# Second block's attention: turned queries and keys straight from the products, two heads at a time on parts of TensorE's array

## What is computed

```python
def odd_mixer(h_lat, h_ctx, ...):             # 256 tokens and 256 context tokens
    z = h @ w_in                               # latents cq (384), ckv (256), shared kr (32), gates
    q = (rms_norm(cq) @ w_uq).reshape(n, 8, 64 + 32)     # nope 64, rope 32 columns
    q = concat(q[..., :64], rope(q[..., 64:]))
    kv = (rms_norm(ckv) @ w_ukv).reshape(512, 8, 64 + 64)
    k = concat(kv[..., :64], broadcast(kr, 8 heads))     # one rotated part for all heads
    v = kv[..., 64:]
    p = softmax(q @ k.T * 96 ** -0.5)          # 256 queries, 512 keys, 8 heads
    o = p @ v                                  # 8 x 64 columns
    return concat(o, gb * conv(gc * hh)) @ w_out
```

## Time and profile before

| what | value |
|---|---|
| time, median of 3 runs | 2270.16 us |
| the 3 runs | 2269.73, 2270.16, 2275.33 us |
| span of the profiled execution | 2267.3 us |
| PE busy | 1983.1 us, 87% of the span |
| DVE busy | 999.4 us, 44% |
| ACT busy | 750.1 us, 33% |
| read from memory | 640.31 MB, 283 GB/s over the span |

### The profile page before, as it was taken

How to read it: one execution, slowest core, us unless ns; L and a number is a source line. 1 busy time by engine, 2 the same in 40 slices (tenths; PEclk the granted TensorE clock), 3 DMA queues, 4 the chain that set the end, 5 groups by cost and what they waited for, 6 DMA issues and landing times.

```text
span 2267.3 us, 37964 instructions
## 1 busy us (share of the span) xinstructions
PE 1983.1 (87%) x16424; PEld 1484.3 (65%) x16424; DVE 999.4 (44%) x1906; ACT 750.1 (33%) x1336; POOL 14.4 (1%) x30
## 2 busy tenths in 40 slices
PE   6999899989898999765565668999999999999998
PEld 5778765444444767544444445878888878788886
DVE  3445522222221656311101105655677756557776
ACT  3344400000000645100000004655455456655544
POOL 0000000000000000000000000000000000000000
PEclk9999999999999999888878878999999999999999
DMA  9868489999999445799999996434545543355551
GB/s 404 334 251 345 148 346 428 428 427 426 428 427 426 170 149 223 282 425 427 427 426 425 427 423 254 149 118 181 203 174 192 196 163 144 118 191 213 195 191 56
DMA packets 49203, 643.79 MB, mean 284 GB/s; under 512 B 5600, under 2 KB 5872, under 8 KB 10256
## 3 DMA queue, kind: packets, MB, share of 16 engines
q1 hardware_dynamic: 46080, 624.56, 68.4%
q0 software_dynamic: 2960, 16.82, 1.9%
HBM read 640.31 MB, written 1.05 MB: 283 GB/s over the span
## 4 chain that ended last, share of the span: by engine, by line
PE 64%; DMA 28%; DVE 4%; ACT 2%; issue 2%; SPq 0%; DVEq 0%; ACTq 0%
PE bank L985 61%; DMA ring<-in_stream 28%; PE bank L993 3%; ACT ring L1921 0%; ACT weights_high L1734 0%; DVE ring L2507 0%; DVE weights_low L2765 0%; ACT tokens_high_low L2085 0%; DVE arena L2865 0%; ACT arena L1767 0%; ACT arena L1756 0%; ACT arena L2051 0%; DVE odz_low L2259 0%; DVE tokens_low L2617 0%; DVE arena L2216 0%
## 5 line engine op out<-in xcount | busy, mean ns | idle before, releaser
L985 PE MATMUL bank<-ring,arena 128*32 128x128 f32 (+5 forms) x7668 | 618.3, 379 | 201.9 <-DMA ring<-in_stream 194.5
L985 PEld LDWEIGHTS bank<-ring,arena 128*32 128x32 f32 (+2 forms) x7668 | 371.1, 135 | 420.3 <-DMA ring<-in_stream 204.8
L2765 DVE TENSOR_TENSOR weights_low<-ring,weights_high 128x1024 fp32r<-128x1024 f32 (+2 forms) x288 | 343.3, 1193 | 257.6 <-ACT weights_high L1734 254.8
L1734 ACT ACTIVATE weights_high<-ring 128x1024 fp32r<-128x1024 f32 (+2 forms) x288 | 297.7, 1035 | 276.3 <-PE bank L985 255.0
L985 PE MATMUL bank<-weights_high,tokens_high_low 128*128 128x512 f32 x960 | 313.8, 398 | 6.3 <-DVE tokens_high_low L2777 4.5
L2425 DVE TENSOR_TENSOR arena<-arena,bank 128x256 f32<-128x256 f32 (+1 forms) x64 | 22.7, 354 | 438.5 <-PE bank L985 438.5
L985 PEld LDWEIGHTS bank<-weights_high,tokens_high_low 128*128 128x128 f32 x960 | 181.0, 188 | 51.8 <-issue 7.4
L1882 ACT ACTIVATE arena<-bank 128x256 f32<-128x256 f32 (+1 forms) x64 | 21.2, 331 | 580.0 <-PE bank L985 580.0
L1734 ACT ACTIVATE arena<-bank 128x256 f32<-128x256 f32 (+6 forms) x218 | 84.5, 414 | 347.6 <-PE bank L993 288.9
L985 PE MATMUL bank<-weights_low,tokens_high_low 128*128 128x512 f32 x480 | 187.9, 392 | 0.0
L985 PE MATMUL bank<-tokens_high_low,weights_high 128*128 128x512 f32 x512 | 178.7, 398 | 2.0 <-DVE tokens_high_low L2777 1.9
(11 more groups left out here) (252 smaller groups left out, 2197.2 us busy)
## 6 DMA issues: line engine op xcount, KB each, us to landing
ring<-in_stream SPq DMA_DIRECT2D x290, 2048.0 KB, 20.1
ring<-in_stream SPq DMA_DIRECT2D x24, 512.0 KB, 9.1
arena<-in_stream POOLq DMA_DIRECT2D x10, 1024.0 KB, 7.2
x<-in_x_in SPq DMA_DIRECT2D x1, 2048.0 KB, 9.1
arena<-in_od_pack POOLq DMA_DIRECT2D x1, 1024.0 KB, 5.1
x<-in_stream POOLq DMA_DIRECT2D x1, 1024.0 KB, 13.2
arena<-in_stream POOLq DMA_DIRECT2D x2, 512.0 KB, 6.8
arena<-in_gains POOLq DMA_DIRECT2D x2, 512.0 KB, 9.7
```

The source lines that it names most:

```text
L985: ins = pe.matmul(o, lhsT, rhs, start=start, stop=stop)
L1734: ins = act.activation(o, i, ACT.Copy)
L2765: dve.tensor_tensor(dst, whole, high.bitcast(F32), ALU.subtract).then_inc(sig, 1)
```

## The change

Head by head turning of queries and keys is gone. The 64 unrotated columns of the queries (`uqn`) and keys (`ukT`) are now computed with the weights stationary and the tokens moving, so that they come out with the head's columns on partitions, the even head of a pair in PSUM rows 0 to 63 and the odd one in rows 64 to 127. Only the rotated part of the queries (`uqr`, 32 columns for each head) is computed with tokens on partitions, rotated by DVE, and turned 128 columns at a time (`odqrT`, 4 turns); the keys' shared rotated part is copied four times side by side and turned (`odkrT`, 4 turns). Values (`uv`) are products of their own.

A unit is now a pair of heads and 128 queries, 8 in all. Scores of two units are issued together: 4 products on 64-row parts of the array, then 4 on 32-row parts that add the rotated part. They take 4 banks; turned weights have 3, the output has one. DVE divides the exponentials by their sum (`divide`) before they are turned. In the output the values are stationary, one head in each column half, and the result comes out turned, so that ACT and DVE write its high and low parts straight to the mix's input. The convolution's part of `cat1` (8 turns) now stands ahead of the attention, and `mix1` starts with it. One transfer (`load_extra(1, 1)`) moves on GpSimd's queue from behind the attention to the front of it.

The core of the diff:

```diff
-ATT_LAGS = [("s", 0), ("t", 3), ("o", 5)]
-ATT_LAGS_ACT = [("t", 3), ("s", 0), ("o", 5)]
-S_BUFS = 4
+OD_LAGS = [("s", 0), ("t", 3), ("o", 4)]
+OD_LAGS_ACT = [("t", 3), ("o", 4), ("s", 0)]
+OD_LAGS_DVE = [("s", 0), ("divide", 1), ("o", 4)]
+OD_S_BUFS = 3
+OD_EARLY_WEIGHTS = 7
-OD_UNITS = [(h, t) for t in range(TT) for h in range(OD_HEADS)]
+OD_PAIRS = OD_HEADS // 2
+OD_UNITS = [(j, t) for t in range(TT) for j in range(OD_PAIRS)]
+def od_steps(lags):
+    return [(kind, u, step) for step, found in enumerate(steps_of(len(OD_UNITS), lags)) for kind, u in found]
+def od_banks(kind, u):
+    if kind == "s":
+        return [(("s", v, e), 2 * (v % 2) + e) for v in (u, u + 1) for e in range(2)] if u % 2 == 0 else []
+    if kind == "t":
+        return [(("t", u, e), 4 + (2 * u + e) % 3) for e in range(2)]
+    return [(("o", u), 7)]
...
@@ TensorE: products
-            for p in range(2):
-                for t in range(TT):
-                    b.vacant("uq", (p, t))
-                    product("uq", (p, t), lambda k: od_cqt[:, k, t * P:(t + 1) * P],
-                            lambda k: uq[:, k, p * 384:(p + 1) * 384], 3, 384)
+            for n in range(2):
+                b.vacant("uqn", n)
+                for pair in range(2):
+                    for k in range(3):
+                        for e in range(2):
+                            mm(bank("uqn", n)[64 * e:64 * e + 64, pair * SEQ:(pair + 1) * SEQ], uq[:, k, 2 * (2 * n + pair) + e, 0:64],
+                               od_cqt[:, k, :], k == 0, k == 2, fills("uqn", n) if (pair, k, e) == (1, 2, 1) else None)
...
+            for j in range(OD_PAIRS):
+                b.vacant("ukT", j)
+                for k in range(2):
+                    for e in range(2):
+                        mm(bank("ukT", j)[64 * e:64 * e + 64, :], ukv[:, k, 2 * j + e, 0:64], od_ckvt[:, k, :], k == 0, k == 1,
+                           fills("ukT", j) if (k, e) == (1, 1) else None)
...
@@ TensorE: attention
+                for key, _ in od_banks("s", u):
+                    b.vacant("odatt", key)
+                for v in (u, u + 1):
+                    j, t = OD_UNITS[v]
+                    for e in range(2):
+                        r = slice(64 * e, 64 * e + 64)
+                        mm(bank("odatt", ("s", v, e))[:, :], od_qn[r, j, t * P:(t + 1) * P], od_kn[r, j, :], True, False)
+                for v in (u, u + 1):
+                    j, t = OD_UNITS[v]
+                    for e in range(2):
+                        first = KR * ((2 * j + e) % 4)
+                        r = slice(first, first + KR)
+                        mm(bank("odatt", ("s", v, e))[:, :], od_qr[r, j // 2, t * P:(t + 1) * P], od_kr[r, :], False, True,
+                           fills("odatt", ("s", v, e)))
...
+                for n in range(4):
+                    for e in range(2):
+                        cols = slice(64 * e, 64 * e + 64)
+                        mm(bank("odatt", ("o", u))[cols, 0:P], od_v[:, n, (2 * j + e) * 64:(2 * j + e + 1) * 64], od_pt[u % 2][:, e, n, :],
+                           n == 0, n == 3, fills("odatt", ("o", u)) if (n, e) == (3, 1) else None)
...
@@ ScalarE
+                if (kind, step) == ("o", OD_EARLY_WEIGHTS):
+                    for n in range(EARLY_SPLIT):
+                        z_split("mix1", 0, n)
...
@@ VectorE
+                elif kind == "divide":
+                    for e in range(2):
+                        b.drained("odatt", ("s", u, e))
+                    steps.do(dve.reciprocal(rl[:, cols], l[:, cols]))
+                    for e in range(2):
+                        s = od_s[u % OD_S_BUFS][:, e, :]
+                        dve.tensor_scalar(s, s, rl[:, 2 * u + e:2 * u + e + 1], None, ALU.mult).then_inc(sem("od_weights"), 1)
```

More of the change, by code:

```diff
@@ L303, in _tickets @@
             stage("conv", [(t, d) for t in range(TT) for d in range(2)])
-            stage("uq", [(p, t) for p in range(2) for t in range(TT)])
-            stage("ukv", [(p, t) for p in range(2) for t in range(4)])
-            stage("odkT", OD_HEADS)
-            stage("odqT", OD_HEADS // 2)
-            stage("odatt", pipeline(len(OD_UNITS), ATT_LAGS))
-            stage("cat1", KD)
+            stage("uqr", 1)
+            stage("uqn", 2)
+            stage("ukT", OD_PAIRS)
+            stage("odkrT", 1)
+            stage("uv", 4)
+            stage("odqrT", 1)
+            stage("cat1", KD - OD_PAIRS)
+            for kind, u, _ in od_steps(OD_LAGS):
+                for key, bank in od_banks(kind, u):
+                    BANK_OF["odatt", key], TURN_OF["odatt", key] = bank, turns[bank]
+                    turns[bank] += 1
             stage("mix1", [(c, t) for c in range(2) for t in range(TT)])
@@ new lines, in _ @@
+            for t in range(4):
+                b.vacant("uv", t)
+                product("uv", t, lambda k: od_ckvt[:, k, t * P:(t + 1) * P], lambda k: ukv[:, k, :, 64:P], 2, 512)
+            used("ukv", 0)
+            pe.wait_ge(sem("od_rope"), 1)
+            b.vacant("odqrT", 0)
+            for n in range(2):
+                for t in range(TT):
+                    turn(bank("odqrT", 0)[:, (n * TT + t) * P:(n * TT + t + 1) * P], od_q[:, t, n * P:(n + 1) * P],
+                         sig=fills("odqrT", 0) if (n, t) == (1, TT - 1) else None)
@@ L2025, in _ @@
-            for h in range(OD_HEADS):
-                b.filled("odkT", h)
-                copy(od_kt[0:OD_DIM, h, :], bank("odkT", h)[0:OD_DIM, :], frees("odkT", h))
-            for kind, u in pipeline(len(OD_UNITS), ATT_LAGS_ACT):
+            b.filled("uqr", 0)
+            copy(od_q[:, :, :], bank("uqr", 0)[:, :].rearrange("p (t n) -> p t n", t=TT), frees("uqr", 0))
+            for n in range(2):
+                b.filled("uqn", n)
+                copy(od_qn[:, 2 * n:2 * n + 2, :], bank("uqn", n)[:, :].rearrange("p (j q) -> p j q", j=2), frees("uqn", n))
@@ new lines, in _ @@
+            for j in range(OD_PAIRS):
+                b.filled("ukT", j)
+                copy(od_kn[:, j, :], bank("ukT", j)[:, :], frees("ukT", j))
+            b.filled("odkrT", 0)
+            copy(od_kr[:, :], bank("odkrT", 0)[:, :], frees("odkrT", 0))
+            for t in range(4):
+                b.filled("uv", t)
+                copy(od_v[:, t, :], bank("uv", t)[:, :], frees("uv", t))
+            for k in range(KD - OD_PAIRS):
+                b.filled("cat1", k)
+                copy(c1_hi[:, k, :], bank("cat1", k)[:, 0:SEQ], sem("cat_hi"))
@@ L2327, in mix1 @@
             def mix1():
-                for k in range(KD):
-                    cat_low(1, k, bank("cat1", k)[:, 0:SEQ], SEQ, frees("cat1", k))
-                    if k == 1:
-                        for n in range(EARLY_SPLIT):
-                            z_split("mix1", 0, n)
                 for c in range(2):
@@ L2701, in _ @@
[L2701 to L2708 removed]
+            b.drained("uqr", 0)
```

221 lines of the change are left out of this document (100 added, 121 removed).

## The result

The changed kernel takes 2276.61 us (median of 20 executions, 2272.54 to 2281.43 without one disturbed execution of 2905 us), the kernel before 2270.62 us (20 executions). The ratio is 1.0025, 95% interval 1.0018 to 1.0032: 5.7 us slower by the ratio, where I had forecast 3.2 us (2273 us) and called anything within 0.3% the same; the interval just reaches past 0.3%.

A forecast was written before the change was run, and what follows sets the result against it. PE was taken to pace the mixer, and the mixer the program. Terms: -4.4 + 7.4 - 3.2 = -0.2 us, plus 3.4 for the clock, +3.2 on the span of 2267.3; with 2.9 to the median, 2273 us, range 2262 to 2281.

The forecast's parts named there:

- The products and turns: Mixer before attention: PE work sums to 28.8 us, plus 1.3 for splits; attention starts at 841.2, 4.4 us earlier.
- The stands: PE waits before the second, third and fourth score blocks for exponentials to release banks: 4.8, 4.9 and 2.5 us.
- Attention at full clock: First scores to attention's end: 42.7 us against 35.3 before, 7.4 more, despite PE's own work of 27.2.
- The 3.2 us behind it: Between attention and mix: the 3.2 us of last division, turns and split of `cat1` disappear.
- The first mix product: Sign at the mixer's end: it comes at 884 to 887 us with no wait for `cat1`.
- One us of the mixer is one us of the program: Experts' stream and the layers behind shift with the mixer's end, one to one; otherwise the prediction is wrong as a whole.
- The clock: Attention: granted clock falls at the first two stands, perhaps the third; 1.7 us for each of two blocks, +3.4 us.
- the order of the lists: Attention: what binds in the count, rather than ACT's load of 2.6 us for a unit against PE's 3.4.
- The page that I weighed: Packing speeds up TensorE but not emptying PSUM, a possible bottleneck; by it the loss would be ACT's load.
- PE stays the bound: Rival, attention: hand-overs hidden by the lag of 3 steps, 32 to 36 us; -9 us, 2261; chance 0.19.
- The clock stays low for most of the attention: Rival, attention: each us of PE work at 0.50 costs 1 us; 10 us low gives 2280; chance 0.16.
- 32-row parts do not run together: Rival, score blocks: serial rotated products add 9.8 us; +13, 2283, or in twos 2277; chance 0.11.

The follow-up runs named there:

- the kernel with idle products: Changed kernel plus 5, 5 and 2 products that nothing reads, ahead of the score blocks of units 2, 4 and 6; ratio 0.9991 to the kernel before.
- the block in order of units: Changed kernel with all four products of a score block's first unit issued before the second's, still asking for four banks; ratio 1.0067 to the kernel before.
- the one other order that was run: Changed kernel with only the three lists reordered: turns two steps behind scores and ahead of them, outputs three; ratio 1.0006 to the kernel before.
- the unit by unit kernel: Changed kernel with scores issued for one unit at a time, asking for two banks instead of four; ratio 0.9975 to the kernel before.
- the kernel without rotated products: Changed kernel without the 16 rotated score products on 32-row parts, so scores lack the rotated part; 2266.09 us, ratio 0.9985 to the kernel before.
- the kernel with the values moved: Changed kernel with the four value products moved in twos ahead of the score blocks of units 2 and 4; ratio 0.9969 to the kernel before.

## Why the forecast held, and where it was off

**The products and turns** were 4.1 us shorter, forecast 4.4. **The stands** were forecast at 4.8, 4.9 and 2.5 us and are 4.53, 4.52 and 2.24. **Attention at full clock** was forecast at 42.7 and was 42.2 in the kernel with idle products. **The 3.2 us behind it** are gone. **The first mix product** comes at 890.8 us, behind the 884 to 887 I had named as a sign: 0.7 us because the convolution starts later in this execution, the rest by the mixer's own excess of 2.9 us. The small errors inside the attention cancel, which is luck: a block takes 3.06 us at full clock instead of 2.85, 0.8 us more over the four, while the stands add up to 11.3 us instead of 12.2. **One us of the mixer is one us of the program**: over eleven kernels it holds within 2.1 us but for one. That one, the block in order of units, is 15.2 us slower with a mixer 11.0 longer. Its profiled execution was its fastest (2278.62 us, mean clock 0.956); the other five took 2283 to 2294 us at a mean clock of 0.946 to 0.950. Their mean clock suggests that they ran longer at the low clock; in which stretch, no trace shows.

**The clock was mis-sized**: 1.7 us for each of two blocks, 3.4 in all, where it took 2.6, 2.1 and 1.6 us of three, 6.3 in all, inside the bounds of 0 to 8.6. I had counted on a part of the slow time lying in the stand; the first fall came late in the stand (mean clock 0.60 from 848 to 850 us, the block starting at 849.80), the third just ahead of its block (0.57 from 872 to 874, the block starting at 872.55), and most of each block ran slow. I also called the third fall a "perhaps". These 2.9 us are what lies between the forecast of +3.2 and the measured +6.1 of the mixer.

**What binds** the text put down to "the order of the lists", and in another place to the block that "holds all four score banks". The second is right: the one other order that was run is worth 1.3 us at full clock, asking for two banks at a time 7.3. The page that I weighed, the Trainium skill's TensorEngine Tiling (Array Packing), Performance Considerations, points at the emptying of PSUM. Here that is no limit: in the unit by unit kernel, from 845 to 880 us, ScalarE is busy for 22.32 of 35 us and VectorE for 22.27, PE for 32.30. Nearer is what the same page of the Trainium skill says under Restrictions and Gotchas: "Different row tiles write to different PSUM banks". The trace fits that: the four 32-row products that run together have four banks, and it is for those that the next block waits. No run puts two row parts into one bank.

**The rivals.** *PE stays the bound*: no, it stood 11.3 us; but the unit by unit kernel comes near this case, at -5.7 us with 5 us more of PE's work, where I had given -9. *The clock stays low for most of the attention*: no, PE worked at it for 2 x 6.3 = 13 of 48 us; the block in order of units did come out so, low for all of 850 to 870 us, at +15. *32-row parts do not run together*: no, 1.07 us for four. By the Trainium skill, TensorE: Matmul & The Clock Gate, Part 3, I had estimated 1.12; the trace agrees.

## What to carry to other kernels

Where each row part of a packed step fills a bank of its own, as here, before grouping more products into one step follow a bank round its whole loop (products, reductions, exponentials, release) and see whether PE has other work for that time; half the packing with half the banks was 12 us better here. Where a stand can't be avoided, put useful products of another stage into it rather than ahead of it: it pays twice, for the products and for the clock. When the trace shows equal blocks of unequal length, read the clock before looking for another wait.

## What the runs showed of the chip

A stand of PE can cost more than its length. Behind stands of 4.5 us blocks of 3.06 us took 5.68 and 5.19, behind 2.24 us 4.61 and 4.66; behind stands of 1.03 to 1.18 us none was longer. Stands of 2.25 us had no such effect in the kernel without rotated products (block of 1.99 us) and in the block in order of units (4.30 us), nor had one of 2.16 us in the kernel with the other order, so the length alone does not decide. Nor does the fall always lie inside the stand: behind the 2.24 us in the kernel with the values moved, the clock was still 1.00 from 863 to 864 us and fell while PE was busy again.

Being busy did not bring the clock back in every case: in the block in order of units PE was busy for 9.53 of 10 us (850 to 860) and the granted clock stayed at 0.50, while the changed kernel's blocks, with four 32-row products together where that one has two, each left the low clock before their end (5.68, 5.19 and 4.61 us, where 2 x 3.06 = 6.1 would be low throughout). I did not vary this by itself, so whether it is the packing that counts or when the stand began stays open.

Four products of 512 columns on 32-row parts took 1.07 us behind products on 64-row parts, the change between the part sizes included; two of them took 2.15 - 1.00 = 1.15 us (a unit's scores less half of the 1.99 us for two units' 64-row products), so the second pair adds nothing that can be seen. What the change of part size costs by itself, no run separates.
